# A kernel of 52 stages: between two stages the engines meet once in place of twice

## The reference

```python
p_lat = (_layer_norm(h_x) * (1.0 + sc_l[:, None]) + sh_l[:, None]) @ w_in[l]
pv_l, u_l, fh_l, g_l = _split_proj(p_lat)
y_rc, y_rl = _rwkv_branch(...)      # chunked recurrence, two directions, states 64x64
o_hc, o_hl = _hgrn_branch(...)      # gated recurrence, two directions
pool_l = _pool_branch(pv_l, True, pool_w[l], pool_scale[l])
mix_l = jnp.concatenate([pool_l, y_rl, o_hl], axis=-1) * jax.nn.silu(g_l)
new_x = _layer_norm(ALPHA * h_x + gt_l[:, None] * (mix_l @ w_out[l])) * ln_g[l] + ln_b[l]
```

## Time and profile before

| | us |
|---|---|
| median of 3 runs | 3032.05 |
| the three runs | 3029.53, 3032.05, 3037.12 |
| the profiled execution, its own time | 3028.03 |
| its span, from the first to the last instruction | 3026.2 |
| TensorE's mean granted clock over the span | 0.917 |

### The profile page before, as it was taken

How to read it: one execution, slowest core, us unless ns; L and a number is a source line. 1 busy time by engine, 2 the same in 40 slices (tenths; PEclk the granted TensorE clock), 3 DMA queues, 4 the chain that set the end, 5 groups by cost and what they waited for, 6 DMA issues and landing times. The chain is left out here.

```text
span 3026.2 us, 60369 instructions
## 1 busy us (share of the span) xinstructions
PE 2564.8 (85%) x25174; PEld 2128.5 (70%) x25174; DVE 1470.6 (49%) x2420; ACT 947.8 (31%) x1584; POOL 702.2 (23%) x433
## 2 busy tenths in 40 slices
PE   7956696685786798967777899999998899799998
PEld 3845584583674587856776788888887666588886
DVE  6787685434435775352636244214414366543241
ACT  3243124222223432441223232112224333332232
POOL 0011100230322131203030422222242200544444
PEclk9977697896897899988998999999999999899999
DMA  6511150000004352200002111211113310523222
GB/s 256 194 57 43 46 181 30 3 4 1 3 4 149 126 191 84 98 31 3 2 3 112 57 56 62 74 51 62 68 65 118 110 28 1 204 88 100 89 100 85
DMA packets 62996, 229.81 MB, mean 76 GB/s; under 512 B 6336, under 2 KB 12736, under 8 KB 60736
## 3 DMA queue, kind: packets, MB, share of 16 engines
q1 hardware_dynamic: 62784, 226.72, 21.4%
HBM read 212.01 MB, written 13.63 MB: 75 GB/s over the span
## 5 line engine op out<-in xcount | busy, mean ns | idle before, releaser
L2259 POOL TENSOR_TENSOR b_wl<-b_stage,b_wh 128x1024 fp32r<-128x1024 f32 (+1 forms) x72 | 186.4, 2589 | 478.4 <-ACT b_wh L2255 478.4
L2558 DVE SCALAR_TENSOR_TENSOR f_xr<-f_ps,cols,f_xr 128x511 f32<-128x511 f32 (+1 forms) x132 | 83.2, 658 | 327.5 <-ACT f_xr L2551 327.5
L2259 POOL TENSOR_TENSOR c_wl<-c_stage,c_wh 128x1024 fp32r<-128x1024 f32 (+1 forms) x68 | 182.3, 2680 | 216.1 <-ACT c_wh L2255 216.1
L2390 PE MATMUL f_ps<-h_h,b_wl 128*128 128x256 f32 (+1 forms) x672 | 226.4, 337 | 0.0
L2390 PE MATMUL f_ps<-h_h,b_wh 128*128 128x256 f32 (+1 forms) x672 | 226.3, 337 | 0.0
L2255 ACT ACTIVATE b_wh<-b_stage 128x1024 fp32r<-128x1024 f32 (+1 forms) x72 | 81.5, 1132 | 461.3 <-PE f_ps L2390 404.9
L2390 PE MATMUL f_ps<-h_l,b_wh 128*128 128x256 f32 (+1 forms) x672 | 225.9, 336 | 0.0
L2255 ACT ACTIVATE c_wh<-c_stage 128x1024 fp32r<-128x1024 f32 (+1 forms) x68 | 77.3, 1136 | 259.7 <-PE f_ps L2390 232.8
L2259 POOL TENSOR_TENSOR a_wl<-a_stage,a_wh 128x1024 fp32r<-128x1024 f32 x33 | 85.9, 2603 | 267.3 <-ACT a_wh L2255 267.3
L2390 PEld LDWEIGHTS f_ps<-h_h,b_wh 128*128 128x128 f32 x672 | 127.6, 190 | 13.7
L2390 PEld LDWEIGHTS f_ps<-h_l,b_wh 128*128 128x128 f32 x672 | 127.5, 190 | 13.3
(11 more groups left out here) (694 smaller groups left out, 6843.9 us busy)
## 6 DMA issues: line engine op xcount, KB each, us to landing
b_stage<-in_ffn_up SPq DMA_DIRECT2D x44, 512.0 KB, 3.2
c_stage<-in_ffn_up SPq DMA_DIRECT2D x44, 512.0 KB, 3.2
first_stage<-in_w_in SPq DMA_DIRECT2D x33, 512.0 KB, 3.7
a_stage<-in_ab_w SPq DMA_DIRECT2D x25, 512.0 KB, 3.5
p_hgrn_side_w<-in_ada_w SPq DMA_DIRECT2D x12, 1024.0 KB, 5.0
b_stage<-in_ffn_down SPq DMA_DIRECT2D x16, 704.0 KB, 4.0
c_stage<-in_ffn_down SPq DMA_DIRECT2D x16, 704.0 KB, 4.1
a_in_side_w<-in_ada_w SPq DMA_DIRECT2D x8, 1024.0 KB, 7.2
```

Source lines behind the costliest of these rows:

```text
L2259: self.nc.gpsimd.tensor_tensor(self.wl[:, slot, :w], self.stage[:, slot, :w], self.wh[:, slot, :w].bitcast(F32), ALU.subtract).then_inc(se ...
L2390: done = self.nc.tensor.matmul(out[s][:, :tn], w, x[:, k, t0:t0 + tn], start=k == 0 and n == 0, stop=k == job.kt - 1 and n == 2)
L2558: nc.vector.scalar_tensor_tensor(out, b[:, :n - 1], self.tap(part, 0, i), out, ALU.mult, ALU.add).then_inc(self.before_ok[part], 1)
```

## The change

Leaving a stage closes its block, which is still a meeting of all engines, but no longer clears anything. The list of the stage's semaphores is kept in `Stage.left`. When the next stage opens its block, it has already taken its own semaphores, so that they have other numbers; only then POOL clears the numbers left by the stage before and gives them back. No meeting follows that clear: the other four engines go from the first meeting straight into the next block, and POOL follows when it has cleared. At the end of the program the last stage's numbers are cleared and one meeting is held, as before. The other lines of the kernel are the same, 13 lines further down at the stages.

```diff
     def sem(self, name):
+        assert not self.opened
         s = self.nc.alloc_semaphore(f"{self.name}_{name}")
...
     def block(self):
+        Stage.clear(self.nc)
+        self.opened = True
         return self.mem.enter_context(self.nc.Block())
+
+    @classmethod
+    def clear(cls, nc):
+        if cls.left:
+            nc.clear_and_free_semaphores(cls.left)
+            cls.left = []
 
     def __exit__(self, *exc):
         self.mem.close()
         if exc[0] is None:
-            self.nc.clear_and_free_semaphores(self.sems)
-            self.nc.all_engine_barrier()
+            assert self.opened
+            Stage.left = self.sems
         return False
...
         second(nc, d, t, out, x_dram, qkv, p_ab, root, tall, weights_kept, weights, keep)
+    Stage.clear(nc)
+    nc.all_engine_barrier()
```

More of the change, by code:

```diff
@@ L25 @@
 class Stage:
+    left = []
     def __init__(self, nc, name):
         self.nc, self.name = nc, name
-        self.mem, self.sems, self.credits = ExitStack(), [], None
+        self.mem, self.sems, self.credits, self.opened = ExitStack(), [], None, False
     def __enter__(self):
@@ L4048, in build @@
 def build(nc, d, out):
+    Stage.left = []
     with ExitStack() as mem:
```

## The result

| | kernel before | changed kernel |
|---|---|---|
| median, first set of runs | 3032.0 us (3028.1 to 3037.1, 6 runs) | 3002.6 us (2999.6 to 3009.9, 6 runs) |
| ratio, first set | | 0.9907, 95% interval 0.9891 to 0.9923 |
| ratio, second and third set | | 0.9917 (0.9900 to 0.9934); 0.9912 (0.9896 to 0.9929) |
| spans of three profiles each | 3026.2, 3031.3, 3024.5 us | 3008.1, 3004.5, 3000.2 us |

The forecast was 3010 us with a range of 3000 to 3021, 22 us under before. The first set is 29 us under by its medians and 28 by the ratio, the three sets have a mean ratio of 0.9912, which is 27 us. The means of the three spans are 3027.3 and 3004.2 us, 23.1 apart.

The account below looks back on a forecast made before the run. Stage ends were taken as always on the path, so passages are lost time: -25.0 + 1.6 + 0.2 + 0.7 + 0.4 = -22.1 us, 3005.9 profiled, 3009.9 with 4.0 us added for the median; forecast 3010, range 3000 to 3021.

Parts of the forecast that it names:

- The passages (-25.0): Stage ends: time from POOL's first release to its second, 0.49 us each, is saved at 51 ends: -25.0 us.
- A pair of drain and clear (0.16): On POOL: each added pair costs 0.14 to 0.20 us, taken as 0.16; there are 98 more.
- POOL late in `rwkv_inv` (+1.6): Starts of two `rwkv_inv` stages: others wait for POOL's first product, delayed by the clears; 0.7 and 0.9, together +1.6 us.
- The cover in `gdn_inv` (nothing): Starts of two `gdn_inv` stages: PE's idle matmuls at half clock, 3.75 us, hide POOL's lateness; priced at nothing.
- The short modulation stage (+0.2): Two `modulation` stages in 1.1 us: POOL's four clears make it come last to the next meeting, +0.2 us.
- the last passage (+0.7): Kernel's end: six clears in place of one between the last two meetings, +0.7 us.
- Late passages (+0.4): Six passages where POOL's drain starts late or is long, 1.5 us together; some shows elsewhere, +0.4 us.
- the clears on the path: Rival at stage starts: POOL's lateness delays most stages, all 98 clears count, +15.7 us, total 3023; 8%.
- freed time that isn't time: Rival at stage starts: engines kept by something else, part of the 25 us stays; half gives 3020; 6%.
- slower loops: Rival at TensorE's loop branches: moved loops reload code, up to 87 us, 3097; 2%.
- the statement that inside a stage nothing changes its distance from the start: Inside stages: nothing is in flight at the meeting, so work and loads keep their distance from the stage's start.
- The clock rival: TensorE at stage starts: shifted clock changes, 1.8 us each; five more at full clock 3001, five fewer 3019; 6% either side.

Follow-up runs that it names:

- split clears: Changed kernel with each stage's semaphore numbers cleared in up to four lists, 332 drain-and-clear pairs in place of 150; ratio 0.9933 to the kernel before.
- bands: Changed kernel with semaphore numbers taken in turn from two fixed bands, 52 clears in place of 150; ratios 0.9913 and 0.9897 to the kernel before.
- the meeting put back: Changed kernel with the second meeting of all engines put back behind the clear; ratio 1.0045 to the kernel before.
- the third meeting: Kernel before with one more meeting behind the second at each of the 52 stage ends; ratio 1.0063 to the kernel before.
- the bare meeting added: Changed kernel with one more meeting at each stage end, ahead of the clears; ratio 0.9962 to the kernel before.

## Why the prediction was right, and where not

**The passages (-25.0).** Right. Three profiles of before have 25.0, 25.0 and 24.9 us, the changed kernel has none, and the first work of a stage comes 0.16 us behind the release on PE and DVE (forecast 0.14). The price of 355 ns that the Trainium skill gives for a round (the same section) would have given 18.1 us, too little because a passage also held a drain and a clear; for the round alone its size fits (0.345 and 0.350).

**A pair of drain and clear (0.16).** Right: 0.146, at the low end of the 0.14 to 0.20.

**POOL late in `rwkv_inv` (+1.6).** Right at the start of the stages: POOL 0.81 and 0.93 us behind the release (forecast 0.85 and 1.0), and TensorE's first real product at 2.98 and 3.10 us, in place of 2.32 in both, so 0.66 + 0.78 = 1.4 us. In the pair of profiles above with the clock alike it arrives at the end of the second stage in full. For the first no such pair of these two kernels exists, since the lower stretches fall differently there.

**The cover in `gdn_inv` (nothing).** Right: the first real product stands 3.84 us behind the release in both stages, in before, in the changed kernel and with split clears. `rw_trans`, also priced at nothing, has its slack: with split clears POOL starts on it 0.92 and 1.30 us behind the release (0.14 in before) and is done at 5.0 and 5.4, and the first reads come at 5.9 us or later in both kernels.

**The short modulation stage (+0.2) and the last passage (+0.7).** Right: 0.18 in each of three profiles, and 1.37 - 0.69 = 0.68.

**Late passages (+0.4).** Nothing of it is seen. The drain of 199 ns has its like in the row of clears ahead of `gdn_inv` (198 ns, the maximum above), and is hidden there by the idle matmuls.

Traced terms, in place of the forecast's -22.1: -25.0 + 1.4 + 0.2 + 0.7 = -22.7 us. The means of three spans give -23.0. Of the rivals, the clears on the path fell by bands and by the split clears; freed time that isn't time fell with the starts at 0.16 us; slower loops didn't come: the branches read as in the earlier trace rows, and q8 loads as in the earlier trace rows:

```profile
L2182 PEldq COMPARE_BRANCH  x74: 76/208/226, 92.1 to 2990.2; - x74
```
```profile
q8 instruction: 166, 2.72, 0.4%
```

**The step that failed is the statement that inside a stage nothing changes its distance from the start,** with its sign for "wrong", stage lengths that differ by more than 0.5 us. They do. Eleven of 52 stages lie apart between the kernels by more than 0.4 us beyond the scatter of three profiles each: the first `gdn_inv` -4.7, `rwkv_front` before the first `rwkv_inv` +3.4, that `rwkv_inv` +2.3, others -2.6, -1.5, +1.3, -1.2, and the rest below 1. Ten of them went the way of the granted clock: shorter where TensorE spent less time at the lower level, longer where more. The clock rival had the mechanism, and its ±9 us didn't come, since the parts cancel: the eleven sum to -1.3 us, all 52 to +1.2. Of the +1.2 the late starts of POOL (1.4 + 0.2) are more than all, so the rest sums to -0.4. The mean of the clock over the span of the profiles (0.917, 0.916, 0.919 before; 0.918, 0.916, 0.919 after) shows nothing of it.

**From the profiled run to the median.** I added 4.0 us, the distance in the runs before. The profiled executions of before lie 2.8 us under the medians in the mean (3029.1 against 3031.9 over four sets), those of the changed kernel 1.1 above theirs (3006.0 against 3004.9). So the median fell by 27 and the profiles by 23. With a spread of 7 to 8 us between three profiles of one kernel the 4 us aren't resolved. The record has the granted clock of every timed run, and it points to the clock: 0.9179 in the mean of the changed kernel's 18 runs, 0.9164 in 39 of before. Among runs of one kernel a clock higher by 0.001 goes with a time shorter by 1.6 us, so the 0.0015 would be an estimated 2.4 us. That is a correlation and not a cause shown; for the meeting put back (0.9145) and the third meeting (0.9122), added to their passages, the same sum gives 17 and 25 us where 14 and 19 were measured. So the forecast of 22 was right on the terms that the traces show, and some 4 of the 27 us measured stand in no term of it.

Two numbers of the prediction need a word. Half of the freed time staying gives 3020 only without the other terms; with them it is 3022. And POOL and PE start 0.14 and 0.16 us behind the release, which the text rounds to 0.1.

## What to carry to other kernels

A meeting of all engines between two stages is lost time one for one; count the round and what stands between two rounds, here 0.35 us and 0.146 for each drain and clear. Work that one engine does behind the release is nearly free unless others wait for that engine at the start of the next stage, or the stage is shorter than that work: look for those stages and price them alone. And when a change shifts the starts of stages, compare stage lengths over several profiles of both kernels: a clock's gains and losses in single stages can repeat and still say nothing on the change as a whole.

## What was unexpected of the hardware

The stretches at which TensorE is granted the lower of its two levels (1.2 in place of 2.4 GHz) are not all scattered afresh in each execution. In the first `gdn_inv` stage they begin 8.5 and 15.3 us behind the stage's release in all three profiles of before, whose absolute starts differ by 1.7 us, and none begins in the first 58 us in those of the changed kernel and of bands, whose starts differ by 15 us. That speaks for stretches that follow what the engine did before, rather than a moment of their own. In the changed kernel, with half a microsecond less between stages, one stage is 4.7 us shorter and another 3.4 longer, with the same instructions. The idle time between stages isn't shown to be what decides: with the meeting put back and with a third meeting one stretch begins at 13.0 and 13.2 us, and with the bare meeting added none does before the stage's end. Other stages differ even between profiles of one kernel (the second `rwkv_inv` stage: 87.2, 90.3 and 87.4 us in before, 88.7, 93.1 and 88.0 in the changed kernel), so this holds for some places and not for all. What the engine has to do for it to come out the better way wasn't tried.

A short drain and clear on POOL take 41 and 44 ns (the medians with split clears), and a pair added costs 0.146 us. The longest clear takes 326 ns in the changed kernel; with that list of numbers cleared in quarters, the longest of all 332 clears takes 110 ns.
